# First loads in smaller pieces, and the first convolution ahead of a weight split, in a four-network transformer kernel

## Chip, cores and metric

The kernel runs on one core of one Trainium2 chip. The metric is device time in microseconds (us); three runs gave 1028.97, 1029.12 and 1029.18, median 1029.12. Engines are called by the profile's names: PE is TensorE, DVE is VectorE, ACT is ScalarE, POOL is GpSimd, SP is the engine that issues most transfers.

## What is computed

Two transformer stages over 256 tokens of 1024 features, in float32. The first stage is a short-convolution mixer, a SwiGLU network, sliding-window attention and a second SwiGLU network; the second stage is a SwiGLU network, a mixture of latent attention and retention, and a last SwiGLU network. Each branch sits between RMS norms and is added to the residual. The change lies in the mixer, at the very start:

```python
# h: (256, 1024); w_in: (1024, 3 * 1024); conv_w: 3 taps for each feature
n = h * rsqrt(mean(h * h) + 1e-6) * pre_norm
b, c, u = split(n @ w_in, 3)          # gate, carrier, value
y = b * causal_conv(c * u, conv_w)    # three taps along the tokens
h = h + rmsnorm(y @ w_out, post_norm)
```

(The names b, c, u are this sketch's own.)

## The kernel before

**Tiling.** The 256 tokens are two row tiles of 128 (t = 0 and 1). Weights come from memory as a stream of chunks, each 128 x 1024 floats (512 KB). To keep float32 accuracy at a faster matmul rate, each chunk is split in two: ACT copies it, rounded, to `w_high` (`split_high`, L1370) and DVE subtracts, giving `w_low` (`split_low`, L1693). The activations are split the same way (`xTh`, `xTl`). A product then takes three passes, high x high, high x low and low x high (L2097, L2098, L2101 for the mixer's inputs; L2108, L2112, L2116 elsewhere). The split chunks go round a ring of 12 slots.

**The mixer** has 8 blocks of 128 features (384 weight columns each, three chunks), and for each row tile and block: G, the input product; a gate copied by ACT (L1484) and multiplied by DVE (L1849, `act`); T, two transposes on PE (L2125) followed by the convolution, ACT's copy `cv` (L1495), ACT's first tap `yT` (L1500), DVE's other taps (L1873) and its product with the gate (L1875); Y, the split of the result into `aTh` (ACT, L1517) and `aTl` (DVE, L1884); D, the output product.

**The start.** Block 0's input product (`first`, L2142) does not use the split: it multiplies the unsplit turned x (`hg`, after the norm's gain, L1716) with unsplit weights `first_w` in plain float32, 8 k tiles of 384 columns for each row tile, while the first chunks are loaded and split. SP issues the loads in this order: left half of x of tile 0 (256 KB), chunks 0 and 1 of `first_w`, right half of x of tile 0, chunk 2 of `first_w`, x of tile 1, then `raw` chunk 0, h of tile 0 (needed for the norm's root), `raw` chunks 1 to 3, four `early` chunks, h of tile 1. ACT issues one load, `consts` (the identity for the transposes and the gains and taps together, 109.5 KB). Before the data is there PE runs 11 matmuls on a zeroed tile (`WARM_UPS`, L2131). DVE waits for `consts` and then for each half of x; `first` waits for a half of `hg` and for each chunk of `first_w`.

**The order of the work** is written by hand: one function calls the same steps for all engines and each engine takes its own part. Chunks are numbered from 0 after those of `first_w`; chunks 0 to 2 are block 1's input weights, 3 is block 0's output weights, 4 to 6 are block 2's input. The transposes of block 0 are not a step of their own on PE but stand inside block 1's input product, ahead of the k tile that `TURN_IN_PRODUCT` names for the row tile:

```python
if ph.mixer and b == 1 and kt == TURN_IN_PRODUCT[t]:
    turn_gated(t, 0, ph)
```

SP reloads a `raw` buffer once the chunk in it is split (L1116).

Of the kernel before, what the change touches and what calls it, by code (L numbers as in the profile page):

```python
# [35 lines left out]
P = 128  # L36
D = 1024
# [83 lines left out]
TURN_IN_PRODUCT = (2, 2)  # L121
FIRST_TURN = 4
TABLES_AFTER = 24
WARM_UPS = 11
# [99 lines left out]
def walk_first_block(step):  # L224

    step("turn", 0, 0)
    step("first", 0)
    step("parts", 0, 0)
    step("turn", 1, 0)
    step("first", 1)  # L230
    split(step, 0)
    step("norm", 0)
    split(step, 1)
    step("G", 0, 0, 0)
    split(step, 2)
    step("high", 3)
    step("T", 0, 0, 0)
    step("low", 3)
    step("high", 4)
    step("Y", 0, 0, 0)  # L240
    step("low", 4)
    step("high", 5)


def walk_second_block(step):

    step("G", 0, 1, 0)
    step("low", 5)
# [517 lines left out]
def build(nc, x_in, x_turned, stream, consts_in, table_in, pos_in, posts_in, out):  # L766
    with ExitStack() as ctx:
# [144 lines left out]
        first_loaded = [sem(f"first_loaded{i}") for i in range(FIRST)]  # L912
        first_done1, warm_ready = sem("first_done1"), sem("warm_ready")
        h_loaded = rows2("h_loaded")
        xt_left, xt_right, xt1_loaded = sem("xt_left"), sem("xt_right"), sem("xt1_loaded")
# [4 lines left out]
        d_quarter, end_m, end_r, end_w = sem("d_quarter"), sem("end_m"), sem("end_r"), sem("end_w")  # L920
# [9 lines left out]
        halo_zero = sem("halo_zero")  # L930
# [3 lines left out]
        q_done0 = sem("q_done0")  # L934
# [7 lines left out]
        x_done0, u_done0 = sem("x_done0"), sem("u_done0")  # L942
# [19 lines left out]
        e_ready, lg_ready = sem("e_ready"), sem("lg_ready")  # L962
# [73 lines left out]

        def branch_done(eng, t, k, half):
# [23 lines left out]
        def proj_done(eng, j, t):  # L1061
            if t == 0:
                eng.wait_ge(q_done0, j + 1)
# [3 lines left out]
        def x_product(eng, i, t):  # L1067
            if t == 0:
                eng.wait_ge(x_done0, i + 1)
# [11 lines left out]
        def _(sp):  # L1081
            def start(ph):
                def first_weights(i):
                    sp.dma_start(first_w[:, i * CHUNK:(i + 1) * CHUNK], stream[i]).then_inc(first_loaded[i], 16)
# [68 lines left out]
        def _(pool):  # L1153
# [8 lines left out]
            def start(ph):  # L1162
                link(pool.memset(half_neg, -0.5))
                link(pool.memset(one_neg, -1.0))
                for i in range(3):
                    pool.memset(cv[i][:, 0:2], 0.0).then_inc(halo_zero, 1)
# [33 lines left out]
            def log_decays():  # L1200
# [13 lines left out]
                pool.tensor_scalar(lg, lg_p, -1.0, None, ALU.mult).then_inc(lg_ready, 1)  # L1214
# [116 lines left out]
            def finish(ph):  # L1331
# [4 lines left out]
                for half in range(2):  # L1336
                    pool.wait_ge(h_ready[0], 2 * FFN4.index + half + 1)
                    weighted(0, slice(512 * half, 512 * half + 512)).then_inc(end_w, 1)
                pool.wait_ge(end_m, 1)
                pool.tensor_tensor(rr[0], ms[0], half_neg[:, 0:1], ALU.pow).then_inc(end_r, 1)  # L1340
                pool.wait_ge(end_w, 1)
# [1308 lines left out]
```

## Time and profile before

| | |
|---|---|
| median of three runs | 1029.12 us |
| the profiled execution, its own time | 1029.98 us |
| its span in the profile | 1028.2 us |
| PE busy | 1020.1 us, 99% of the span |
| DVE busy | 684.2 us, 67% |
| ACT busy | 567.0 us, 55% |
| PE's share of the chain that ended last | 96% |
| DMA, mean over the span | 198 GB/s |

The span is what the profile shows between the first and the last instruction; 1.8 us of the profiled execution's time lie outside it. Matmuls are pipelined and their ends are modelled, so PE's busy time hides short pauses; the starts of successive matmuls show them better. An answer for a stretch gives each engine's busy time in it, the granted clock of PE and the share and rate of the transfers.

### The profile page before, as it was taken

Reading aid. Unit: us, or ns where it says so; the run is one execution under the profiler, and the core shown is the slowest. Engines: PE = TensorE matmul, PEld = TensorE weight load, DVE = VectorE, ACT = ScalarE, POOL = GpSimd, SP = SyncE. Lnnn points to the kernel's source line nnn. Section 1 sums busy time; section 2 is a strip of 40 time slices with the busy share of each in tenths; the row PEclk is TensorE's granted clock in tenths of the full one; section 3 lists DMA queues with packets and bytes.
Section 4 is the critical chain, followed back from the end, with each engine's and each line's share of the span. In section 5 each row is a group of like instructions: output and inputs, shape, how many; then the busy total and the mean of one; then the engine's idle time right before and its main releaser. Section 6 shows DMA issues by size and latency. Waiting matters only on the chain.

```text
span 1028.2 us, 14332 instructions
## 1 busy us (share of the span) xinstructions
PE 1020.1 (99%) x4783; PEld 839.0 (82%) x4783; DVE 684.2 (67%) x1034; ACT 567.0 (55%) x925; POOL 137.1 (13%) x219
## 2 busy tenths in 40 slices
PE   9999999999999999999999999999999999999997
PEld 6999888888877778888888888888887688888886
DVE  5777856656788985656668565656787685655643
ACT  5665654545567864444556454454676854454542
POOL 1100450000143152000014000000400220000002
PEclk9999999999999999999999999999999999999999
DMA  9575577566643467667576775757643355757551
GB/s 364 174 238 187 184 226 242 179 226 200 211 145 126 146 225 249 217 196 243 178 235 210 233 222 188 245 176 243 207 168 122 98 171 176 239 184 238 187 175 46
DMA packets 104174, 203.56 MB, mean 198 GB/s; under 512 B 52976, under 2 KB 57472, under 8 KB 104128
## 3 DMA queue, kind: packets, MB, share of 16 engines
q1 hardware_dynamic: 101952, 197.44, 59.0%
q0 software_dynamic: 1888, 5.17, 1.8%
q8 instruction: 25, 0.41, 0.2%
q10 hardware_dynamic: 288, 0.37, 0.1%
q14 instruction: 21, 0.17, 0.1%
HBM read 187.20 MB, written 1.05 MB: 183 GB/s over the span
## 4 chain that ended last, share of the span: by engine, by line
PE 96%; DVE 1%; ACT 1%; DMA 0%; POOL 0%; issue 0%; POOLq 0%; DVEq 0%; SPq 0%; ACTq 0%
PE pG L2108 16%; PE pG L2116 16%; PE pG L2112 16%; PE pD L2108 11%; PE pD L2112 11%; PE pD L2116 11%; PE pG L2097 2%; PE pG L2101 2%; PE pG L2098 2%; PE pT L2125 1%; PE pD L2142 1%; PE pD L2101 1%; PE pD L2097 1%; PE pD L2098 1%; PE pG L2422 1%; PE pG L2125 1%
## 5 line engine op out<-in xcount | busy, mean ns | idle before, releaser
L1693 DVE TENSOR_TENSOR w_low<-raw,w_high 128x1024 fp32r<-128x1024 f32 x340 | 410.3, 1225 | 195.8 <-ACT w_high L1370 185.7
L1370 ACT ACTIVATE w_high<-raw 128x1024 fp32r<-128x1024 f32 x340 | 354.7, 1056 | 207.0 <-PE pG L2116 135.9
L2108 PE MATMUL pG<-w_high,xTh 128*128 128x512 f32 x712 | 220.0, 390 | 0.0
L2112 PE MATMUL pG<-w_high,xTl 128*128 128x512 f32 x712 | 219.6, 389 | 0.0
L2116 PE MATMUL pG<-w_low,xTh 128*128 128x512 f32 x712 | 219.4, 390 | 0.2 <-DVE w_low L1693 0.2
L2116 PEld LDWEIGHTS pG<-w_low,xTh 128*128 128x128 f32 x712 | 133.6, 188 | 28.2 <-DVE w_low L1693 0.6
L2112 PEld LDWEIGHTS pG<-w_high,xTl 128*128 128x128 f32 x712 | 133.6, 188 | 28.1 <-DVE xTl L1739 0.2
L2108 PEld LDWEIGHTS pG<-w_high,xTh 128*128 128x128 f32 x712 | 133.3, 188 | 27.3
L1484 ACT ACTIVATE gate<-pG,stat 128x256 f32<-128x256 f32 x102 | 48.4, 474 | 140.1 <-PE pG L2116 124.0
L2108 PE MATMUL pD<-w_high,aTh 128*128 128x512 f32 x348 | 107.8, 391 | 0.0
L2116 PE MATMUL pD<-w_low,aTh 128*128 128x512 f32 x348 | 107.5, 390 | 0.0
L2112 PE MATMUL pD<-w_high,aTl 128*128 128x512 f32 x348 | 107.4, 390 | 0.0
L1856 DVE SCALAR_TENSOR_TENSOR act<-pG,stat,gate 128x256 f32<-128x256 f32 x88 | 43.9, 499 | 70.7 <-ACT gate L1484 70.4
L2116 PEld LDWEIGHTS pD<-w_low,aTh 128*128 128x128 f32 x348 | 65.2, 188 | 14.2 <-DVE w_low L1693 0.7
L2112 PEld LDWEIGHTS pD<-w_high,aTl 128*128 128x128 f32 x348 | 65.3, 188 | 13.8
L2108 PEld LDWEIGHTS pD<-w_high,aTh 128*128 128x128 f32 x348 | 64.8, 188 | 12.1
L2108 PE MATMUL pD<-w_high,xTh 128*128 128x512 f32 (+1 forms) x144 | 47.1, 408 | 0.0
L2112 PE MATMUL pD<-w_high,xTl 128*128 128x512 f32 (+1 forms) x144 | 44.3, 389 | 0.0
L1259 POOL TENSOR_SCALAR stat<-stat 128x1 f32<-128x1 f32 x8 | 2.8, 356 | 308.9 <-ACT junk L1466 308.7
L2116 PE MATMUL pD<-w_low,xTh 128*128 128x512 f32 (+1 forms) x144 | 44.0, 387 | 0.0
L1266 POOL DMA_DIRECT2D xF<-hg x32 | 18.0, 568 | 174.1 <-DVE hg L1768 173.9
L1509 ACT ACTIVATE aTh<-aF 128x256 fp32r<-128x256 f32 x80 | 32.9, 411 | 11.3 <-DMA aF<-aB 10.3
(312 smaller groups left out, 1112.9 us busy)
## 6 DMA issues: line engine op xcount, KB each, us to landing
raw<-in_stream SPq DMA_DIRECT2D x340, 512.0 KB, 4.6
aF<-aB SPq DMA_DIRECT2D x320, 32.0 KB, 2.6
post<-in_posts POOLq DMA_DIRECT2D x5, 512.0 KB, 4.7
early<-in_stream SPq DMA_DIRECT2D x4, 512.0 KB, 13.1
xF<-hg SPq DMA_DIRECT2D x32, 64.0 KB, 2.5
xF<-hg POOLq DMA_DIRECT2D x32, 64.0 KB, 2.3
first_w<-in_stream SPq DMA_DIRECT2D x3, 512.0 KB, 5.8
h<-in_x SPq DMA_DIRECT2D x2, 512.0 KB, 11.9
```

The lines of the kernel that those rows point to most:

```text
L1370: sc.activation(w_high[:, slot(static):slot(static) + CHUNK], raw_of(static), ACT.Copy).then_inc(w_high_done, 1)
L1484: sc.activation(gate[t][:], gate_bank(ph, t, b)[:, 0:256], ACT.Copy if ph.mixer else ACT.Silu, scale=rr[t]).then_inc(gate_ready[t], 1)
L1509: sc.activation(act_parts(ph, t, b)[0][:].rearrange("p k (a r) -> p k a r", a=4), turned_act(ph, t, b), ACT.Copy).then_inc(ah_ready[t], 1)
L1693: ve.tensor_tensor(w_low[:, slot(static):slot(static) + CHUNK], raw_of(static), w_high[:, slot(static):slot(static) + CHUNK].bitcast(F32), ...
L1856: ve.scalar_tensor_tensor(dst, up, rr[t], by, ALU.mult, ALU.mult).then_inc(act_ready[t], 1)
L2097: pe.matmul(dst, ah, hi, start=start, stop=False)
L2098: pe.matmul(dst, ah, lo, start=False, stop=False)
L2101: return pe.matmul(dst, al, hi, start=False, stop=stop)
L2108: pe.matmul(dst, ah, w_high[:, where:where + n], start=start, stop=False)
L2112: pe.matmul(dst, al, w_high[:, where:where + n], start=False, stop=False)
L2116: mm = pe.matmul(dst, ah, w_low[:, where:where + n], start=False, stop=stop)
L2125: return pe.transpose(dst, src, ident)
```

## The change

- SP's first loads become smaller: x of tile 0 as two quarters (128 KB each) and its right half; `first_w` as six pieces of 512 columns (256 KB) in place of three chunks; x of tile 1 as two halves. The identity (64 KB) is loaded by SP between the halves of x of tile 1, and ACT's own load is the gains and taps alone (45.5 KB).
- DVE makes the left half of `hg` in two quarters. PE starts `first` with the first quarter and the first piece. DVE makes `hg` of tile 1 ahead of `xTl` of tile 0. The first block still takes tile 0 whole and then tile 1.
- 9 zero matmuls in place of 11.
- The transposes of block 0, tile 0, stand ahead of k tile 3 instead of k tile 2.
- On ACT the high part of chunk 3 comes behind the convolution's `cv` and `yT`, and that of chunk 4 behind `aTh`; chunk 5 follows the gate.
- Some semaphores are merged into one with counts (`proj_done0`, `end_weights`, `halo_and_logs`), which frees the numbers for the new pieces; the order of what is waited for stays.

```diff
-TURN_IN_PRODUCT = (2, 2)
+TURN_IN_PRODUCT = (3, 2)
-WARM_UPS = 11
+WARM_UPS = 9
+PIECE = 512
...
 def walk_first_block(step):
 
-    step("turn", 0, 0)
+    step("opening", 0)
     step("first", 0)
+    step("opening", 1)
+    step("first", 1)
     step("parts", 0, 0)
-    step("turn", 1, 0)
-    step("first", 1)
     split(step, 0)
     step("norm", 0)
     split(step, 1)
     step("G", 0, 0, 0)
     split(step, 2)
-    step("high", 3)
     step("T", 0, 0, 0)
-    step("low", 3)
-    step("high", 4)
+    split(step, 3)
     step("Y", 0, 0, 0)
-    step("low", 4)
-    step("high", 5)
+    split(step, 4)
...
     step("G", 0, 1, 0)
-    step("low", 5)
+    split(step, 5)
     split(step, 6)
...
-                sp.dma_start(xt[0][:, 0:512], x_turned[0, :, 0:512]).then_inc(xt_left, 16)
+                left_quarter, second_quarter, right_half = slice(0, 256), slice(256, 512), slice(512, D)
+                load_x(0, left_quarter, xt_first)
                 first_weights(0)
                 first_weights(1)
-                sp.dma_start(xt[0][:, 512:D], x_turned[0, :, 512:D]).then_inc(xt_right, 16)
+                load_x(0, second_quarter, xt_second)
                 first_weights(2)
-                sp.dma_start(xt[1][:], x_turned[1]).then_inc(xt1_loaded, 16)
+                load_x(0, right_half, xt_right)
+                for i in (3, 4, 5):
+                    first_weights(i)
+                load_x(1, slice(0, 512), xt1_loaded)
+                sp.dma_start(consts[:, C_ID:C_FEATS], consts_in[:, C_ID:C_FEATS]).then_inc(ident_loaded, 16)
+                load_x(1, right_half, ident_loaded)
...
-                sc.dma_start(consts[:, 0:C_ROPE], consts_in[:, 0:C_ROPE]).then_inc(ident_loaded, 16)
+                sc.dma_start(consts[:, C_FEATS:C_ROPE], consts_in[:, C_FEATS:C_ROPE]).then_inc(xt_first, 16)
...
-                ve.wait_ge(ident_loaded, 16)
...
+            def opening(t, ph):
+                if t == 0:
+                    ve.wait_ge(xt_first, 32)
+                    gained_quarter(0, 0).then_inc(warm_ready, 1)
+                    ve.wait_ge(xt_second, 16)
+                    gained_quarter(0, 1).then_inc(hg_ready[0], 1)
+                    ve.wait_ge(xt_right, 16)
+                else:
+                    ve.wait_ge(xt1_loaded, 16)
+                    gained_quarter(1, 0).then_inc(warm_ready, 1)
+                    gained_quarter(1, 1).then_inc(hg_ready[1], 1)
+                    ve.wait_ge(ident_loaded, 32)
+                gained(t, GAIN[0], 1, xt[t][:, 512:D])
...
-                pe.wait_ge(ident_loaded, 16)
 
             def first(t, ph):
 
+                pe.wait_ge(warm_ready, t + 2)
                 for kt in range(KT):
-                    if kt % 4 == 0:
-                        pe.wait_ge(hg_ready[t], kt // 4 + 1)
+                    if kt in (2, 4):
+                        pe.wait_ge(hg_ready[t], kt // 2)
                     if t == 0:
-                        for i in range((kt * MIX.cols + CHUNK - 1) // CHUNK, ((kt + 1) * MIX.cols - 1) // CHUNK + 1):
+                        for i in range((kt * MIX.cols + PIECE - 1) // PIECE, ((kt + 1) * MIX.cols - 1) // PIECE + 1):
                             pe.wait_ge(first_loaded[i], 16)
...
+                if t:
+                    pe.wait_ge(ident_loaded, 32)
```

How the instructions stand on an engine before and in the changed kernel, at three places. SP's queue at the start, before (`xt_56` is x of tile 0, `xt_57` of tile 1, `h_58` the residual of tile 0):

```order
L1092 DMA xt_56<-in_x_turned 128x512
L1084 DMA first_w<-in_stream 128x1024 x2
L1095 DMA xt_56<-in_x_turned 128x512
L1084 DMA first_w<-in_stream 128x1024
L1097 DMA xt_57<-in_x_turned 128x1024
L1087 DMA raw<-in_stream 128x1024
L1090 DMA h_58<-in_x 128x1024
```

and now:

```order
L1089 DMA xt_56<-in_x_turned 128x256
L1086 DMA first_w<-in_stream 128x512 x2
L1089 DMA xt_56<-in_x_turned 128x256
L1086 DMA first_w<-in_stream 128x512
L1089 DMA xt_56<-in_x_turned 128x512
L1086 DMA first_w<-in_stream 128x512 x3
L1089 DMA xt_57<-in_x_turned 128x512
L1107 DMA consts<-in_consts 128x128
L1089 DMA xt_57<-in_x_turned 128x512
L1092 DMA raw<-in_stream 128x1024
```

Six loads stood ahead of the first `raw` chunk; now twelve do, with 64 KB more (the identity, which ACT's load gave up).

ACT from the high part of chunk 1 to the gate of block 1, before:

```order
L1370 ACTIVATE w_high<-raw 128x1024
L1484 ACTIVATE gate_88<-pD,stat 128x256
L1370 ACTIVATE w_high<-raw 128x1024 x2
L1495 ACTIVATE cv_96<-pT 128x128
L1500 ACTIVATE yT_99<-cv_96,consts 128x128
L1370 ACTIVATE w_high<-early 128x1024
L1517 ACTIVATE aTh_80<-yT_99 128x128
L1370 ACTIVATE w_high<-early 128x1024
L1484 ACTIVATE gate_88<-pG,stat 128x256
```

and now:

```order
L1380 ACTIVATE w_high<-raw 128x1024
L1493 ACTIVATE gate_88<-pD,stat 128x256
L1380 ACTIVATE w_high<-raw 128x1024
L1504 ACTIVATE cv_96<-pT 128x128
L1509 ACTIVATE yT_99<-cv_96,consts 128x128
L1380 ACTIVATE w_high<-raw 128x1024
L1526 ACTIVATE aTh_80<-yT_99 128x128
L1380 ACTIVATE w_high<-early 128x1024
L1493 ACTIVATE gate_88<-pG,stat 128x256
```

Each of the splits of chunks 3, 4 and 5 stands one place later against the convolution and the gate; DVE's order in this stretch is the same in both.

PE in block 1's input product of tile 0 (three rows are one k tile), now:

```order
L2122 MATMUL pG0<-w_high_50,xTh0_52 128x384
L2123 MATMUL pG0<-w_low_51,xTh0_52 128x384
L2126 MATMUL pG0<-w_high_50,xTl0_54 128x384
L2150 MATMUL pT0<-consts_63,gate0_88 128x128
L2150 MATMUL pT0<-consts_63,act0_90 128x128
```

Three k tiles stand ahead of the two transposes, where two did; five follow instead of six.

## Rows read from the trace of the kernel before

**Rows 1.** The page: busy time, and the chain that ended last, by engine.

```profile
PE 1020.1 (99%) x4783; PEld 839.0 (82%) x4783; DVE 684.2 (67%) x1034; ACT 567.0 (55%) x925; POOL 137.1 (13%) x219
...
PE 96%; DVE 1%; ACT 1%; DMA 0%; POOL 0%; issue 0%; POOLq 0%; DVEq 0%; SPq 0%; ACTq 0%
```

**Rows 2.** The chain of waits up to 24 us: start us, us, what.

```profile
1.20 4.99 DMA first_w<-in_stream
6.18 0.14 issue
6.32 10.93 PE pD L2142 x32
...
22.84 0.27 DVE act L1849
23.16 0.44 PE pT L2125 x2
```

**Rows 3.** Stretches: engines busy us (count), PEclk, DMA share, GB/s.

```profile
2.00:2.50 0.50, 0.50 (x3) 0.21 (x2) 0.00 (x0) 0.47 (x1) 0.00 (x0) 1.00 0.59 87
10.00:15.00 5.00, 5.00 (x17) 3.02 (x16) 2.52 (x3) 2.78 (x6) 1.15 (x2) 1.00 1.03 410
...
23.15:29.00 5.85, 5.84 (x32) 5.54 (x33) 5.42 (x9) 4.76 (x12) 2.11 (x3) 1.00 0.77 305
29.00:40.00 11.00, 11.00 (x64) 10.57 (x63) 8.54 (x17) 7.22 (x15) 1.18 (x1) 1.00 0.37 121
```

**Rows 4.** Transfers issued in the first 12 us: KB each, median us to landing.

```profile
first_w<-in_stream SPq DMA_DIRECT2D x3, 512.0 KB, 5.8
...
xt<-in_x_turned SPq DMA_DIRECT2D x2, 256.0 KB, 5.1
xt<-in_x_turned SPq DMA_DIRECT2D x1, 512.0 KB, 7.3
consts<-in_consts ACTq DMA_DIRECT2D x1, 109.5 KB, 4.3
```

**Rows 5.** Timeline, start: start us, us, engine, line, count, [idle before <-releaser].

```profile
0.74 0.40 SPq L1092 DMA_DIRECT2D xt<-in_x_turned  x1
1.19 4.87 PE L2131 MATMUL pD<-warm 128*128 128x512 bf16 x11 [1.19 <-DVE warm L1702]
5.10 0.69 DVE L1716 TENSOR_TENSOR hg<-xt,consts 128x512 f32<-128x512 f32 x1 [3.97 <-DMA consts<-in_consts]
...
12.01 1.06 ACT L1370 ACTIVATE w_high<-raw 128x1024 fp32r<-128x1024 f32 x1 [2.48 <-DMA raw<-in_stream]
```

**Rows 6.** Timeline of PE alone, 6.2 to 9 and 9 to 12 us.

```profile
6.32 2.86 PE L2142 MATMUL pD<-first_w,hg 128*128 128x384 f32 x7 [0.26 <-DMA first_w<-in_stream]
...
8.69 3.71 PE L2142 MATMUL pD<-first_w,hg 128*128 128x384 f32 x11
```

**Rows 7.** Timeline, PE, 17 to 24 us.

```profile
18.14 0.27 PE L2125 MATMUL pT<-consts,gate 128*128 128x128 f32 x1
...
21.51 0.62 PE L2108 MATMUL pD<-w_high,aTh 128*128 128x512 f32 x2
```

**Rows 8.** Timeline, ACT, 14 to 24 us.

```profile
16.14 2.05 ACT L1370 ACTIVATE w_high<-raw 128x1024 fp32r<-128x1024 f32 x2
18.56 0.28 ACT L1495 ACTIVATE cv<-pT 128x128 f32<-128x128 f32 x1 [0.37 <-PE pT L2125]
...
20.62 1.05 ACT L1370 ACTIVATE w_high<-early 128x1024 fp32r<-128x1024 f32 x1
```

**Rows 9.** Timeline, DVE, 14 to 24 us.

```profile
16.80 0.34 DVE L1849 SCALAR_TENSOR_TENSOR act<-pD,stat,gate 128x128 f32<-128x128 f32 x1
...
20.29 1.22 DVE L1693 TENSOR_TENSOR w_low<-raw,w_high 128x1024 fp32r<-128x1024 f32 x1
21.63 1.22 DVE L1693 TENSOR_TENSOR w_low<-early,w_high 128x1024 fp32r<-128x1024 f32 x1
22.76 0.34 DVE L1849 SCALAR_TENSOR_TENSOR act<-pG,stat,gate 128x128 f32<-128x128 f32 x1
```

More of the change, by code:

```diff
@@ L911, in build @@
         w_freed = sem("w_freed")
-        first_loaded = [sem(f"first_loaded{i}") for i in range(FIRST)]
+        first_loaded = [sem(f"first_loaded{i}") for i in range(FIRST * CHUNK // PIECE)]
         first_done1, warm_ready = sem("first_done1"), sem("warm_ready")
         h_loaded = rows2("h_loaded")
-        xt_left, xt_right, xt1_loaded = sem("xt_left"), sem("xt_right"), sem("xt1_loaded")
+        xt_first, xt_second, xt_right, xt1_loaded = sem("xt_first"), sem("xt_second"), sem("xt_right"), sem("xt1_loaded")
         ident_loaded, tables_loaded = sem("ident_loaded"), sem("tables_loaded")
@@ L1035, in moved_block, with x_count @@
             return network(ph) * (ph.nb - 1) + b + t + shift * (RING // (ph.cg + ph.kd))
+        def x_count(i):
+            return 3 + i + (1 if i < 3 else 2)
         def branch_done(eng, t, k, half):
@@ L1711, in low, with gained_quarter @@
                 split_low(c, c)
+            def gained_quarter(t, quarter):
+                cols = slice(256 * quarter, 256 * quarter + 256)
+                g = feats[:, 2 * quarter:2 * quarter + 2].unsqueeze(2).broadcast_to([P, 2, P])
+                return ve.tensor_tensor(hg[t][:, cols].rearrange("p (k r) -> p k r", k=2), xt[t][:, cols].rearrange("p (k r) -> p k r", k=2),
+                                        g, ALU.mult)
             def gained(t, col, half, src):
@@ L1745, in turn @@
                     sinks()
-                if p == 0:
-                    for half in range(2):
-                        ve.wait_ge(xt1_loaded if t else (xt_left, xt_right)[half], 16)
-                        gained(t, GAIN[p], half, xt[t][:, 512 * half:512 * half + 512])
-                elif (t, p) not in RIGHT_ONLY:
+                if (t, p) not in RIGHT_ONLY:
                     for half in range(2):
                         gained_half(t, p, GAIN[p], half)
+            def opening(t, ph):
[11 more added lines that the diff above has]
+                gained(t, GAIN[0], 1, xt[t][:, 512:D])
             def left(t, ph):
@@ L2084, in RL @@
                                  xTh[t][:, 4:8, :].rearrange("p k r -> p (k r)").bitcast(F32), ALU.subtract).then_inc(catT_ready[t], 1)
-            steps = dict(start=start, low=low, R=refill, left=left, turn=turn, parts=parts, second=second, second_low=second_low, spread=spread, gain=gain, rest=rest, finish=finish, tail=tail, join=join, G=G, V=V, T=T, Y=Y,
+            steps = dict(start=start, low=low, R=refill, opening=opening, left=left, turn=turn, parts=parts, second=second, second_low=second_low, spread=spread, gain=gain, rest=rest, finish=finish, tail=tail, join=join, G=G, V=V, T=T, Y=Y,
                          rope=rope, QKT=QKT, S=S, N=N, AT=AT, LAT=LAT, KPE=KPE, U=U, RROPE=RROPE, RSUM=RSUM, MT=MT, MS=MS, MN=MN, VC=VC, RT=RT, RM=RM, GNvar=GNvar, GNout=GNout,
```

52 lines of the change are left out of this document (26 added, 26 removed).

## The prediction

> **What bounds the kernel now.** I read the page first: PE is busy 99% of the span and is 96% of the chain that ended last [rows 1]. The change touches only the first 30 us, so next the chain of waits there [rows 2]. It begins with a transfer: the first chunk of `first_w`, issued at 1.20 us, lands at 6.19. At 6.32 PE starts the first product, and then works nearly without a pause, but for one place: the chain leaves PE after the transposes of block 0, goes through the convolution and the splits on DVE, and comes back at 23.16, when `act` of block 1 is ready. How long PE stood there: between the transposes at 18.14 and the output product at 21.51 [rows 7] lie the two transposes (0.11 each by their starts) and six k tiles of three matmuls, so a k tile takes (21.51 - 18.36) / 6 = 0.52, a matmul of 384 columns 0.175 and one of 512 columns 0.233. The output product has six of the latter, so PE was free at 22.91 and waited 0.25. Behind it the stretches show PE busy 5.84 of 5.85 us and 11.00 of 11.00 [rows 3]. So whatever the change does to the moment when PE takes up the transposes of block 1 (23.16) goes through to the end of the kernel, us for us, and nothing else in it does.
>
> **The measure.** A measurement of this kernel can tell about 0.2% from no change, that is 2.06 us. The first product cannot begin before the zero matmuls are done, at 5.0 (below). The whole prize is thus 1.3 us plus the 0.25 us wait.
>
> **Part 1: when the first product starts.** The transfers move 410 GB/s once they run (10 to 15 us [rows 3]), 0.41 MB a us; at 2 to 2.5 us it is 87 GB/s [rows 3]. The start waits for three things.
> (a) The zero matmuls: 11 starting at 1.19 take 4.87 us with the last one's modelled end [rows 5], 0.43 each, so two fewer end 0.85 us earlier, 5.85 - 0.85 = 5.00.
> (b) The first quarter of `hg`. DVE started at 5.10, when `consts` had landed (4.3 us after an issue at 0.74, the moment of SP's first) [rows 4, 5]. In front of it there are now 128 KB less of x and 64 KB less of `consts`: 0.19 MB, 0.47 us at 410 GB/s, so 4.6. A quarter takes half of 0.69 [rows 5]: 4.97.
> (c) The first piece. Ahead of 6.19 lay 0.90 MB (half of x, `consts`, one chunk); now 0.44 MB (a quarter, 45.5 KB, one piece). 0.46 MB less are 1.1 us: 5.1. With the 0.13 us from landing to start that PE needed before, the first product starts at about 5.2.
> The bounds: 5.0, the zero matmuls' end, and 6.3, if landing goes by a fixed latency and not by bytes. I take 5.2, since the steady part of the landings goes by bytes.
>
> **Part 2: how much earlier it ends.** The granted clock column says 1.00 from 2 us on [rows 3], but the spacing says otherwise: 512 columns every 0.43 us is the 1.2 GHz level. Each k tile of the first product is recorded as two matmuls. From 8.69 us 11 of them take 3.71, the last one's modelled 0.49 within: (3.71 - 0.49) / 10 = 0.322 each. The first seven: the last starts at 6.32 + 2.86 - 0.49 = 8.69, five steps of 0.322 back is 7.08, so the first one took 0.76 [rows 6]. PE thus went from the lower to the upper level (2.4 GHz) at about 7.0 us, having worked on the zero matmuls since 1.19. If that moment stays, the product's first us run at half rate: started at 5.2, its first record takes 0.76, the second 0.644 (to 6.60), three are done at 7.16. Before, one was done at 7.08. The gain is 2 x 0.322 - 0.08 = **0.56 us**. Had PE the upper level from the start, it would be the whole 1.1 us.
> The rest of the pieces must keep ahead. At 0.64 us for 256 KB they land at 5.75 (piece 1), 6.05 (second quarter), 6.7, 7.35 (right half), 8.0, 8.6, 9.25, then x of tile 1 at 9.9 and 10.7. PE wants piece 1 at 6.6, piece 2 at 7.5, piece 3 and the right half of `hg` (7.35 + 0.69) at 8.8, the last pieces at 9.4 and 10.1, tile 1 from 11.3 on. At least 0.65 us is in hand everywhere, so nothing waits. `raw` chunk 0 lands, by bytes, at 11.96 as before (ACT took it at 12.01 [rows 5]); behind it nothing changes.
> A rule of the Trainium skill speaks against the pieces. The page "DMA: Bandwidth & Descriptors", section "Rules for kernel authors", wants 1 MiB or more in one transfer for the full rate and calls transfers under 64 KB mostly overhead; the features' 45.5 KB are such a one, and by this page's 2 us of fixed cost for a transfer, were it not overlapped, SP's six further ones would cost 12 us (an estimate). The trace agrees only in part, since 512 KB transfers already run at 410 GB/s here.
>
> **Part 3: from there to 23.16.** The transposes of block 0 stood behind two k tiles and started at 18.14 [rows 7]; now a third stands ahead, 0.52 us. New start: 18.14 - 0.56 + 0.52 = **18.10**, 0.04 earlier. The gain of part 2 is spent on the later place. `act` of block 0 was ready at 16.80 + 0.34 = 17.14 [rows 9], so it binds neither place.
> Behind it the chain is the same on DVE: taps, `low` of chunk 3 at 20.29, `low` of chunk 4 at 21.63, `act` at 22.76 [rows 9]. ACT did the high parts of chunks 2 and 3 back to back from 16.14 to 18.19 and then stood until `cv` at 18.56 [rows 8]. The high part of chunk 3 is moved out of this free stretch, behind `yT`: 19.2 to 20.2, just ahead of DVE's 20.29. That of chunk 4 moves behind `aTh`: it takes the place of the one that started at 20.62 and took 1.05, ends at 21.67, and DVE's split of it can begin at 21.70 instead of 21.63. That is **+0.07 us**. The convolution itself does not come sooner for being put first, since ACT was waiting for PE and not PE for ACT [rows 8].
> Sum at 23.16: -0.04 + 0.07 = **+0.03 us**. PE reaches the place 0.56 us earlier and waits there 0.25 + 0.56 + 0.03 = 0.84 us. Behind it ACT has the high part of chunk 5 one place later than before, with some 0.2 us in hand on DVE and PE; it costs nothing while that cover lasts, and up to 0.2 us if not.
>
> **Part 4: the rest.** The merged semaphores count the same events in the same order; nothing new is waited for: 0. DVE's `xTl` of tile 0 comes behind the two halves of x of tile 1, at about 12.1 instead of 8.8, and is wanted by PE at 16.5: 0. PE's wait for the identity stands at 16.5, with the landing at about 10: 0. SP has six issues more ahead of the `raw` chunks, 0.46 us each (from 0.74 to 1.20 [rows 2, 5]), 2.8 us in all, hidden by the backlog of transfers (the third rival).
>
> The profiled execution had 1029.98 us and a span of 1028.2; the sum gives 1030.0 for it. The median of the runs lies 0.86 below the profiled one; +0.03 on 1029.12 is below a tenth of what can be told, and I forecast **1029.1 us**, chance 0.50.
>
> **Rivals.**
> 1. The gain passes. If the product starts at 5.2 or sooner and PE has the upper level by then, its end is 1.1 us earlier instead of 0.56; 0.59 of it (0.52 for the later transposes, 0.07 for ACT) is spent and 0.5 is left: **1028.6**; with a start at 5.0 and ACT's 0.07 not binding, 1.3 - 0.5 = 0.8, 1028.3. For it: the moment of the rise is a single one in a single execution. Against: rows 6 show it after 6.3. The Trainium skill, "TensorE: Matmul & The Clock Gate", section "Part 1: The HAM clock gate", has this moment shift by half a us from run to run, which speaks for it; no run here shows the shift. Chance 0.24.
> 2. The landing does not come sooner, so the change does not do what it says. At 2 to 2.5 us the transfers are 0.59 busy and move 87 GB/s [rows 3]: the first packets wait on latency. If the first piece lands at 6.2 as before, the gain is 0 and the later place and ACT's order remain: +0.59, **1029.7**. Chance 0.17.
> 3. The number of transfers binds. If `raw` chunks land by their issue, the six issues make each 2.8 us late. DVE's `low` of chunk 1, done just ahead of 16.80 [rows 9], comes at 19.6; PE wants it at 17.6 for its third k tile and has the transposes at 20.1, 2.0 us late. Half of that may be made up behind: +1.0 to +2.0, **1030.6**. Against: a landing 7.3 us after the issue [rows 4] is queueing, not issue. Chance 0.05.
> 4. Slower: the clock. Between the zero matmuls' end and the first product PE may stand longer than the 0.3 us of before, and the lower level may last on. Decides: whether the level rises near 7 us. From the first zero matmul to the rise it took 5.8 us; if the count starts anew with the product at 5.2, the rise is at 11.0, nine records pass at 0.644 and 23 at 0.322, and the product ends at 18.5 against 17.06 (31 steps of 0.322 behind 7.08). With the later transposes and ACT's order that is +2.0: **1031.1**, and over 0.2% with any further wait. Chance 0.04.
>
> **How the numbers follow.** The forecast's case spans 1028.8 to 1029.5. The range takes in rivals 1 and 2 with their bounds (5.0 and 6.3 for the start, 0.2 for ACT's later place) and leaves out rivals 3 and 4: 1028.3 to 1030.0. Faster by over 2.06 us needs more than the prize holds: 0.01. Slower by so much is half of rival 4 and what I have not seen: 0.03. The rest, 0.96, is no change that can be told.
>
> **What would show it.** The first `first` matmul at 5.0 to 5.4; the step from 0.644 to 0.322 us near 7 us; the last of them at about 16.2 instead of 16.76; transposes of block 0 at 18.1, those of block 1 at 23.2 with PE standing 0.8 us ahead of them; ACT's high part of chunk 4 ending at 21.7 and DVE beginning its low part right behind it. The forecast is wrong if the transposes of block 1 start before 22.9 or after 23.5, or if PE pauses anywhere in the first product.

## The result, and the profile after

The changed kernel takes **1030.45 us** (median of 20 runs, 1030.13 to 1031.32), the kernel before 1029.12 beside it (20 runs, 1028.73 to 1029.46): +1.33 us, a ratio of 1.0014 with a 95% interval of 1.0008 to 1.002. That is slower by less than the 2.06 us that were called distinguishable, but it lies outside the range of the prediction, which had 1029.1 (1028.3 to 1030.0). The profiled execution took 1031.06 us with a span of 1029.2.

The page of the changed kernel (its busy lines and the chain by engine) looks like [rows 1]; transfers have gone from 0% of the chain to 1%.

```profile
PE 1019.5 (99%) x4781; PEld 838.6 (81%) x4781; DVE 684.1 (66%) x1036; ACT 565.8 (55%) x925; POOL 138.6 (13%) x219
...
PE 96%; DVE 1%; ACT 1%; DMA 1%; POOL 0%; issue 0%; SPq 0%; POOLq 0%; DVEq 0%; ACTq 0%
```

The chain of waits of the changed kernel up to 25 us (start us, us, what) names the piece: it no longer begins with the first weights but with the third piece, issued at 2.60.

```profile
2.60 5.80 DMA first_w<-in_stream
8.40 0.14 issue
8.54 9.27 PE pD L2167 x28
...
21.70 1.13 DVE w_low L1702
22.83 0.20 DVE aTl L1909
23.03 1.23 DVE w_low L1702
24.26 0.27 DVE act L1874
24.53 0.04 issue
24.57 0.44 PE pT L2150 x2
```

PE's timeline in the changed kernel shows what lies before and behind (start us, us, engine, line, operation, count, and in brackets the idle time ahead).

```profile
3.72 1.49 PE L2156 MATMUL pD<-warm 128*128 128x512 bf16 x3
5.00 1.82 PE L2167 MATMUL pD<-first_w,hg 128*128 128x384 f32 x4
8.54 4.76 PE L2167 MATMUL pD<-first_w,hg 128*128 128x384 f32 x14 [1.73 <-DMA first_w<-in_stream]
...
18.84 0.44 PE L2122 MATMUL pG<-w_high,xTh 128*128 128x384 f32 x1
...
19.47 0.27 PE L2150 MATMUL pT<-consts,gate 128*128 128x128 f32 x1
...
24.57 0.33 PE L2150 MATMUL pT<-consts,gate 128*128 128x128 f32 x1 [0.29 <-DVE act L1874]
```

The product starts at 5.00 instead of 6.32, does two k tiles (four records), and then stands 1.73 us for weight piece 2. The transposes of block 0 are at 19.47 (18.14 in [rows 7]), those of block 1 at 24.57 (23.16 in [rows 2]): +1.41. On ACT the high part of `raw` chunk 0 starts at 13.91 instead of 12.01 [rows 5], 1.90 late:

```profile
13.91 1.06 ACT L1380 ACTIVATE w_high<-raw 128x1024 fp32r<-128x1024 f32 x1 [3.50 <-DMA raw<-in_stream]
...
20.51 1.05 ACT L1380 ACTIVATE w_high<-raw 128x1024 fp32r<-128x1024 f32 x1
21.73 0.31 ACT L1526 ACTIVATE aTh<-yT 128x128 fp32r<-128x128 f32 x1 [0.18 <-DVE yT L1900]
21.95 1.05 ACT L1380 ACTIVATE w_high<-early 128x1024 fp32r<-128x1024 f32 x1
```

Both come from one cause, which the stretches show (columns as in rows 3; the DMA share and GB/s are the last two). The changed kernel:

```profile
2.00:3.00 1.00, 1.00 (x4) 0.44 (x3) 0.00 (x0) 0.47 (x1) 0.00 (x0) 1.00 0.86 253
3.00:4.00 1.00, 1.00 (x4) 0.32 (x3) 0.40 (x1) 0.00 (x0) 0.00 (x0) 1.00 1.04 345
4.00:5.00 1.00, 1.00 (x4) 0.49 (x2) 0.02 (x1) 0.00 (x0) 0.00 (x0) 1.00 0.74 170
5.00:6.00 1.00, 1.00 (x3) 0.57 (x2) 0.00 (x0) 0.00 (x0) 0.00 (x0) 1.00 0.95 284
6.00:8.00 2.00, 0.81 (x3) 0.19 (x1) 0.43 (x1) 0.63 (x1) 0.00 (x0) 1.00 0.95 302
8.00:10.00 2.00, 1.46 (x5) 0.88 (x6) 0.69 (x1) 0.23 (x1) 0.00 (x0) 1.00 0.94 325
10.00:12.00 2.00, 2.00 (x8) 1.08 (x7) 0.23 (x1) 0.40 (x1) 1.26 (x1) 1.00 1.08 419
```

The kernel before, the same stretches up to 10 us:

```profile
2.00:3.00 1.00, 1.00 (x4) 0.44 (x3) 0.00 (x0) 0.47 (x1) 0.00 (x0) 1.00 0.59 108
3.00:4.00 1.00, 1.00 (x4) 0.32 (x3) 0.00 (x0) 0.00 (x0) 0.00 (x0) 1.00 0.87 300
4.00:5.00 1.00, 1.00 (x4) 0.30 (x3) 0.00 (x0) 0.00 (x0) 0.00 (x0) 1.00 1.05 412
5.00:6.00 1.00, 1.00 (x3) 0.15 (x1) 0.69 (x1) 0.18 (x1) 0.00 (x0) 1.00 1.03 408
6.00:8.00 2.00, 1.74 (x5) 1.07 (x5) 0.00 (x0) 0.45 (x1) 0.00 (x0) 1.00 1.04 419
8.00:10.00 2.00, 2.00 (x8) 1.16 (x7) 1.29 (x2) 0.63 (x1) 0.40 (x1) 1.00 1.02 416
```

From 2 to 4 us the changed kernel moves 190 KB more than the kernel before. From 4 to 10 us it moves 782 KB less. Over 2 to 10 us that is 2,306 KB instead of 2,898, and the missing 592 KB are 1.4 us at 410 GB/s. The rest of the 1.9 is unevenness. Each of these transfers is spread over the 16 DMA engines and has landed when the last of the 16 parts has. The parts of `raw` chunk 0 land at 12.76 on average instead of 11.39 (+1.37), the last of them at 13.88 instead of 11.98. The lag stays: the last part comes 0.93 us behind the 14th at this chunk and 0.95 behind it at 25 us, where the two lay 0.2 apart before.

Part of the lost bytes is idle engines (share 0.74 at 4 to 5 us), the larger part is packets that take longer. Packets of 2 KB took 84 ns in the kernel before and 102 on average in the changed one from 6 to 8 us, by single ones of up to 1,048 ns.

### The profile page after: what moved, and what is told of

Its sections match the earlier page's. It is cut to its first block, busy times and chain, and to the rows that moved or that the text cites. A ratio compares the mean times of both kernels' runs of the same rounds, so it can differ in the third digit from the quotient of the medians.

```text
span 1029.2 us, 14335 instructions
## 1 busy us (share of the span) xinstructions
PE 1019.5 (99%) x4781; PEld 838.6 (81%) x4781; DVE 684.1 (66%) x1036; ACT 565.8 (55%) x925; POOL 138.6 (13%) x219
## 4 chain that ended last, share of the span: by engine, by line
PE 96%; DVE 1%; ACT 1%; DMA 1%; POOL 0%; issue 0%; SPq 0%; POOLq 0%; DVEq 0%; ACTq 0%
PE pG L2141 16%; PE pG L2133 16%; PE pG L2137 16%; PE pD L2133 11%; PE pD L2137 11%; PE pD L2141 11%; PE pG L2122 2%; PE pG L2126 2%; PE pG L2123 2%; PE pT L2150 1%; PE pD L2167 1%; PE pD L2126 1%; PE pD L2123 1%; PE pD L2122 1%; PE pG L2449 1%; PE pG L2150 1%
```

## The experiments

All against the kernel before on the same chip. The interval of each ratio is about 0.0009 wide to either side, 0.9 us, so a difference of a few tenths between two kernels rests on the traces, not on their times. And a trace is one execution. The changed kernel, the loads alone (2) and the kernel with only the transposes put back (2) have the very same loads, and `raw` chunk 0 lands at 13.88, 13.24 and 13.83 in their traces. In two traces of the kernel before and that of the order alone (1), again with the same loads, it lands at 11.98, 11.69 and 11.67. A landing that differs by 0.6 us among the cut loads, or by 0.3 among the old ones, shows nothing by itself.

**1. The order of work without the loads.** The kernel before with the later transposes and ACT's new order:

```
-TURN_IN_PRODUCT = (2, 2)
+TURN_IN_PRODUCT = (3, 2)
...
-    step("high", 3)
     step("T", 0, 0, 0)
-    step("low", 3)
-    step("high", 4)
+    split(step, 3)
     step("Y", 0, 0, 0)
-    step("low", 4)
-    step("high", 5)
+    split(step, 4)
...
-    step("low", 5)
+    split(step, 5)
```

> The kernel before with nothing changed but the place of block 0's transposes (behind three k tiles instead of two) and ACT's order of the splits of chunks 3 to 5. If the order costs what the prediction's part 3 says (0.52 us for the place, 0.07 for ACT), block 1's transposes come at 23.75 instead of 23.16 and the time is 1029.7. If the whole loss of the change is a matter of the loads, it is 1029.1.

1029.95 us (1029.66 to 1030.94) beside 1029.35: **+0.60**, ratio 1.0006 (0.9997 to 1.0015). Its trace is best read against a second profile of the kernel before (experiment 7), whose product starts at the same moment. PE, the second profile of the kernel before:

```profile
6.02 5.18 PE L2142 MATMUL pD<-first_w,hg 128*128 128x384 f32 x14
...
17.89 0.27 PE L2125 MATMUL pT<-consts,gate 128*128 128x128 f32 x1
...
22.91 0.33 PE L2125 MATMUL pT<-consts,gate 128*128 128x128 f32 x1
```

PE, the order alone:

```profile
6.00 5.17 PE L2139 MATMUL pD<-first_w,hg 128*128 128x384 f32 x14
...
18.39 0.27 PE L2122 MATMUL pT<-consts,gate 128*128 128x128 f32 x1
...
23.50 0.33 PE L2122 MATMUL pT<-consts,gate 128*128 128x128 f32 x1 [0.30 <-DVE act L1846]
```

The transposes of block 0 are 0.50 later and those of block 1 0.59. The prediction had 0.52 for the place and 0.07 for ACT's order. This half was right by the traces; by time alone +0.60 can't be told from nothing.

**2. The loads without the order of work.** The changed kernel with both of the above put back:

> The changed kernel with the old place of the transposes and ACT's old order: the loads, the quarters of hg and the 9 zero matmuls alone. Loads theory (raw chunk 0 lands near 13.9 us instead of 12.0, everything behind it late): DVE's act of block 0 stays at 18.7, the transposes come right behind it at 19.05 instead of 19.47, and the time is 0.4 to 0.5 below the changed kernel's, 1029.9 to 1030.0. If the order had been the loss, it would be near 1028.6.

1030.54 us (1030.05 to 1031.23): **+1.19**, ratio 1.0012 (1.0003 to 1.0021). `raw` chunk 0 lands at 13.24 (11.98 before), and PE stands twice in its first product, 0.42 and 0.64 us. So the loads alone lose nearly what the changed kernel loses (by 1.19 against 1.33), clear of no change; their gain at the start is gone. The two halves together (0.60 + 1.19) are more than the changed kernel's 1.33. In the loads alone the way from the transposes of block 0 to those of block 1 takes 5.46 us, in the changed kernel 5.11: when `raw` chunk 3 is late, the old order on ACT holds the convolution behind it. To see that by itself, the changed kernel with only the transposes put back:

```
-TURN_IN_PRODUCT = (3, 2)
+TURN_IN_PRODUCT = (2, 2)
```

> The changed kernel with the transposes of block 0 back at the place of before (2, 2), its loads and its ACT order (convolution ahead of the split) kept. If the order on ACT helps once raw chunk 3 is late (its T of block 0 to T of block 1 took 5.11 us in the changed kernel, 5.46 with the old order), the time is 0.9 us over before, 0.3 under the kernel with the new loads alone. If the two orders are worth the same, it stands at the new loads alone, 1.2 over before; if the later transposes are no part of the loss, at the changed kernel's 1.3.

1030.24 us beside 1029.3, ratio 1.0007 (0.9998 to 1.0016). (One of its 12 runs took 2676.77 us, a disturbance that no other run showed; without it the median is 1030.17, +0.87.) Transposes at 19.05 and 24.20, 5.16 apart. The sign is as the first theory has it: convolution first is worth about 0.3 us behind late loads (5.46 - 5.16, and 1.19 - 0.87), but by time alone it can't be told from nothing.

**3. Which of the cuts costs?** The loads alone, with the weights again in three whole chunks (`PIECE = 1024`), x still in quarters:

> As loads_alone, but first_w comes in three whole chunks with 4 KB rows again; x of tile 0 stays in quarters (nine transfers ahead of raw chunk 0 instead of twelve; six before). Row theory (2 KB rows out of 4 KB rows of the stream move at 0.3 MB/us with single packets far over the usual 84 ns): the stall is gone, raw chunk 0 lands at 12.1 to 12.5, the first product starts at 5.0 to 5.6 and does not pause, time 1028.6 to 1029.0. Count theory (the number of transfers and SP's issues delay the rest): half of the delay stays, raw chunk 0 near 13, time near 1029.6.

1029.98 us beside 1029.35: +0.63, ratio 1.0006 (0.9997 to 1.0015); `raw` chunk 0 at 13.06, PE stood 1.26 us for the second chunk. That is what the theory of the count has, and not that of the rows. And the reverse, six pieces, but x of tile 0 in halves:

> As loads_alone (six pieces of weights, old order), but the left half of x of tile 0 comes in one transfer with 2 KB rows, so no transfer has 1 KB rows. whole_chunks showed that the quarters of x by themselves cost about 0.6 us (raw chunk 0 at 13.1). If the two parts add up, this one has raw chunk 0 at about 12.8 and 1029.9; if any small rows do it and the pieces are the larger part, 13.2 to 13.5 and 1030.2; if the quarters alone do it, 12.0 and 1029.2.

1030.70 us beside 1029.28: +1.42, ratio 1.0014 (1.0005 to 1.0023); chunk 0 at 13.63. With neither cut (three chunks, halves of tile 0; x of tile 1 in halves with the identity between them, the features alone on ACT's queue and nine zero matmuls kept):

> As whole_chunks, but x of tile 0 in halves as in the kernel before: neither quarters nor pieces. What is left of the change's loads: x of tile 1 in halves with the identity between them, the features alone on ACT's queue, 9 zero matmuls, hg of tile 1 ahead of xTl of tile 0. If small rows are the loss: raw chunk 0 at 12.0, first product at 5.4 to 5.7 for want of 64 KB of identity ahead of it, time 1028.9 to 1029.3 (before: 1029.35 on this chip). If the number of transfers is (eight ahead of raw chunk 0, six before), 12.5 and 1029.6.

1029.47 us beside 1029.28: +0.19, ratio 1.0003 (0.9994 to 1.0012); chunk 0 at 12.31. Against this last kernel the quarters alone cost 0.44 us more and the pieces alone 1.23. They do not add up: with the pieces in, the quarters bring nothing more (1.19 with them, 1.42 without). Of these four kernels only the two with the pieces stand clear of no change by their times; the pieces are the larger part.

**4. Is it the place of the pieces in memory?** A piece is 2 KB out of each row of 4 KB, a quarter of x 1 KB out of 4. The loads alone with the pieces each together in memory, and the kernel of whole chunks with the quarters so:

```
-sp.dma_start(first_w[:, cols], stream[i * PIECE // CHUNK][:, i * PIECE % CHUNK:i * PIECE % CHUNK + PIECE])
+sp.dma_start(first_w[:, cols], first_in[i])
...
```

> As loads_alone, but the six pieces of weights lie each together in memory (256 KB without a gap) instead of as halves of 4 KB rows; sizes, rows of 2 KB in SBUF, order and number are the same. If the gaps in memory make the packets slow, raw chunk 0 comes at 12.9 to 13.2 instead of 13.9 and 13.2, packets back at 84 ns, and the time falls by 0.5 or more. If the size of a row does it, nothing changes: 1030.4 to 1030.6.

> As whole_chunks, but the two quarters of x of tile 0 lie each together in memory (128 KB without a gap) instead of as quarters of 4 KB rows. If the gaps make them slow, raw chunk 0 comes at 12.2 instead of 13.1 and the time is 1029.2 or less. If it is the 1 KB rows, or the number of transfers, it stays at 1029.8 to 1030.0.

1030.27 us (+0.99, 1.0 to 1.0018) and 1030.23 us (+0.95, 0.9999 to 1.0017), beside 1029.28; chunk 0 at 13.00 and 12.65. With the gaps it was +1.19 and +0.63. The landing of 13.00 lies where the theory of the gaps had it (12.9 to 13.2), but it is not apart from the 13.24 to 13.88 of the same loads with gaps by more than these differ among themselves, and the time did not fall by the 0.5 us that was named. So the gaps are not the main cause; a few tenths can't be excluded.

A third way to ask, six weight transfers of 64 partitions with whole rows of 4 KB:

```
-    cols = slice(i * PIECE, (i + 1) * PIECE)
+    cols, rows = slice(i // 2 * CHUNK, (i // 2 + 1) * CHUNK), slice(64 * (i % 2), 64 * (i % 2) + 64)
...
```

> As loads_alone, but the six weight transfers are 64 partitions each with whole 4 KB rows, two for a chunk: the same number of transfers, issues and bytes as the changed kernel, rows twice as long. Row theory: raw chunk 0 at 12.1 to 12.6 and 1028.7 to 1029.1, like whole_chunks. Count theory: raw chunk 0 near 13.9 and 1029.9 to 1030.0, like loads_alone.

1033.91 us beside 1029.35 (5 runs, 1032.29 to 1035.54): +4.56, ratio 1.0045 (1.0031 to 1.0059). It answers nothing on the question, since with these transfers in the queue all packets were slow: from 4 to 12 us those of 4 KB took 256 to 313 ns on average instead of 159, and those of 2 KB, which belong to x with its 128 partitions, 140 instead of 84. The engines were full (share 1.03):

```profile
8.00:10.00 2.00, 1.14 (x2) 0.00 (x0) 0.69 (x1) 0.22 (x1) 0.00 (x0) 1.00 1.03 213
```

**5. The number of transfers or the size of rows?** The kernel before with six tiny transfers between its first six, nothing cut:

```
 sp.dma_start(xt[0][:, 0:512], x_turned[0, :, 0:512]).then_inc(xt_left, 16)
+sp.dma_start(tiny[0:16, 0:64], consts_in[0:16, 0:64]).then_inc(xt1_loaded, 16)
 first_weights(0)
+sp.dma_start(tiny[0:16, 64:128], consts_in[0:16, 0:64]).then_inc(xt1_loaded, 16)
...
```

> The kernel before with six tiny transfers (16 rows of 256 bytes, 4 KB each) put between its six opening loads on SP's queue; no large transfer is cut. Theory of the count (each further transfer ahead of the raw chunks costs them about 0.25 us): raw chunk 0 lands about 1.5 us later, at 13.2 to 13.6 instead of 11.98, and the kernel takes 0.8 to 1.4 us more. Theory of the short rows: the loads keep their rates (about 410 GB/s from 5 to 10 us), raw chunk 0 lands by 12.3, and the time stands within 0.3 us of before.

1030.1 us beside 1029.3: **+0.80**, ratio 1.0008 (1.0 to 1.0017). Six transfers of 4 KB each, and against 410 GB/s the stretches from 4 to 8 us lose 140, 60 and 158 KB (over 2 to 4 us it moved 200 KB more than the kernel before, so that by 10 us it is 0.2 MB behind, about 0.5 us):

```profile
4.00:5.00 1.00, 1.00 (x3) 0.30 (x2) 0.69 (x1) 0.28 (x1) 0.00 (x0) 1.00 0.84 270
5.00:6.00 1.00, 1.00 (x3) 0.15 (x1) 0.00 (x0) 0.35 (x1) 0.00 (x0) 1.00 0.87 350
6.00:8.00 2.00, 1.13 (x5) 0.68 (x4) 0.00 (x0) 0.00 (x0) 0.00 (x0) 1.00 1.03 331
```

The product starts at 6.93, for want of chunk 0 of `first_w`: 15 of the 16 engines had delivered their part of chunk 0 by 5.10, the last one at 6.80. The changed kernel has the same picture at its piece 2 (15 parts by 6.91, the last at 8.40). `raw` chunk 0 lands at 12.60. The time was as the count has it, the landing was 0.6 sooner than it had it. The other half, three weight transfers of twice the rows:

```
-sp.dma_start(first_w[:, i * CHUNK:(i + 1) * CHUNK], stream[i])
+sp.dma_start(first_w[:, i * CHUNK:(i + 1) * CHUNK].rearrange("p (c n) -> p c n", c=2),
+             first_in[i].rearrange("c p n -> p c n"))
...
```

> The kernel before with its three weight transfers still three, but each of 256 rows of 2 KB (out of two areas in memory) in place of 128 rows of 4 KB; x and the queue as before. Theory of the short rows: a packet of 2 KB does not fill an engine as one of 4 KB does, 4 to 10 us move about 300 GB/s, raw chunk 0 lands at about 13, and the kernel takes 0.6 us more or over. Theory of the count: six transfers as before, raw chunk 0 at 12.0 to 12.3, the time within 0.2 us of before.

1029.64 us: +0.34, ratio 1.0003 (0.9994 to 1.0012); chunk 0 at 12.26, 322 and 342 GB/s at 5 to 6 and 6 to 8 us. The landing is the count's, the time lies between the two theories and can't be told from nothing. The number of transfers counts, with an interval whose lower end is no change; that the rows count too is not shown. That 0.80 + 0.34 = 1.14 is about the 1.19 of the loads alone may be chance, with intervals of 0.9 us.

**6. Does a transfer cost the engines, or does SP hand over too little ahead?** The same six tiny transfers, but among the `raw` chunks:

> The kernel before with the six tiny transfers (4 KB each) between and behind the raw chunks, not between the first six loads. Theory of too short a lead: at that time 3 MB and more are queued, so they cost nothing beyond their bytes; raw chunk 0 at 12.0, the time within 0.2 us of before (they cost 0.8 us among the first loads). Theory that each transfer costs the engines 0.13 us or so wherever it stands: the chunks behind come later by 0.1 to 0.7 us, and the kernel takes 0.3 to 0.8 us more.

1029.43 us beside 1029.23: +0.20, ratio 1.0002 (0.9993 to 1.0011); chunk 0 at 11.70 and `raw` chunks 1 to 3 at 14.33, 15.66 and 17.01, 0.08 to 0.20 later than in the second profile of the kernel before, at 400 GB/s and more. So a tiny transfer costs the engines some 0.05 us there at most, against about 0.13 among the first loads. Then the loads alone with pieces 1, 3 and 5 handed over by ACT:

```
 sc.dma_start(consts[:, C_FEATS:C_ROPE], consts_in[:, C_FEATS:C_ROPE]).then_inc(xt_first, 16)
+for i in (1, 3, 5):
+    cols = slice(i * PIECE, (i + 1) * PIECE)
+    sc.dma_start(first_w[:, cols], stream[i * PIECE // CHUNK][:, i * PIECE % CHUNK:i * PIECE % CHUNK + PIECE]).then_inc(first_loaded[i], 16)
...
```

> The new loads with the old order of work (the kernel 1.19 us over before), with weight pieces 1, 3 and 5 handed over by ACT behind the features, and the rest by SP as before: the same transfers, rows and bytes. Theory that SP hands over too little ahead (one transfer each 0.47 us, while what is queued is short): with two issuers the engines are full from 3 us on, raw chunk 0 lands at 12.2 to 12.6 instead of 13.24, PE's stall before its third k tile is under 0.5 us, and the kernel takes 0.5 to 1.2 us less than with the new loads alone, so 0.0 to 0.7 over before, perhaps less than before. Theory that each short row or each transfer costs the engines: raw chunk 0 stays at 13.0 to 13.5 and the time at 1.0 to 1.3 over before.

1031.02 us beside 1029.23 (1030.65 to 1032.63): **+1.79**, ratio 1.0021 (1.0012 to 1.003). All six weight pieces were issued by 3.6 us, and yet the engines were idle and slow in the same stretches:

```profile
4.00:5.00 1.00, 1.00 (x3) 0.15 (x1) 0.23 (x1) 0.00 (x0) 0.00 (x0) 1.00 0.72 236
5.00:6.00 1.00, 1.00 (x3) 0.61 (x3) 0.00 (x0) 0.00 (x0) 0.00 (x0) 1.00 0.89 224
```

`raw` chunk 0 landed at 13.18, as in the loads alone, though it was issued at 5.88 instead of 7.02, and PE stood 1.56 us before its third k tile. My theory that SP's 0.47 us per issue leaves the engines without work is refuted; the time is above the other theory's range too (+1.0 to +1.3). The changed kernel's own trace says the same: by 4.0 us 1.6 MB were issued and 0.6 MB moved, and yet the next stretch moves 170 GB/s with a share of 0.74. The Trainium skill, "Perfetto Trace Analysis", section "DMA Optimizations", holds out that spreading transfers over the issuing engines may help where the generation of descriptors is the bottleneck; by this run the spreading did not help: it measured 0.6 us more than the loads alone, less than the two intervals can tell apart.

**7. The clock, and the kernel before once more.** The kernel of experiment 3 with neither cut had its profile with TensorE at the lower level (1.2 GHz) for long. PE's timeline there:

```profile
5.85 5.51 PE L2166 MATMUL pD<-first_w,hg 128*128 128x384 f32 x9 [0.64 <-DMA first_w<-in_stream]
```

The same for the kernel with the features first, further below, whose first product has the same instructions:

```profile
4.29 0.81 PE L2131 MATMUL pD<-warm 128*128 128x512 bf16 x3
5.55 5.78 PE L2141 MATMUL pD<-first_w,hg 128*128 128x384 f32 x16 [0.45 <-DMA first_w<-in_stream]
```

In the first one the starts of the nine records lie (5.51 - 0.49) / 8 = 0.63 us apart, the 1.2 GHz level; in the second those of the 16 lie 0.35 apart with two short pauses within, the 2.4 GHz level. There the last three zero matmuls are already at 0.21 instead of 0.43, so the step came at about 4.0 us. In the kernel with neither cut it came at about 10.6, and that execution took 1031.88. With 11 zero matmuls instead of nine:

> The kernel with whole chunks and halves of x, features alone and identity late (0.19 us over before, its profile with TensorE at the lower level until about 10.5 us), with 11 zero matmuls again instead of 9. If the two matmuls hold the clock's rise: it rises by 7.1 us in the profile, no run lies over 1030.2, the median is 1029.2 to 1029.5. If they have nothing to do with it: single runs 1 to 2.5 us over the median come here too, or came there by chance and neither kernel has them in every second set.

1029.27 us beside 1029.23 (1028.96 to 1030.37): +0.04, ratio 1.0001 (0.9992 to 1.001), and the upper level from the first record, at 5.68. The widest run is 1.1 over the median, where the kernel with nine had 2.4; it lies above the 1030.2 that was named. Runs further over their median than 1.1 stand only in kernels with nine zero matmuls: two of the kernel with neither cut, three of the two issuers (1.4 to 1.6), one of the 64 partitions (1.6) and one of six pieces with halves of x (1.2), beside the disturbance of experiment 2. The other profile with a late step, between 8.3 and 10.2 us, is that of the 64 partitions, nine zero matmuls too. In both PE stood (0.6 and 1.0 us) between the last zero matmul and the product with the lower level still on. With eleven, experiment 5's tiny transfers made PE stand 0.87 us, and its product had the upper level at once. That fits the two zero matmuls as what keeps the step from coming late, but the eight other profiles with nine have it between 4.2 and 7.0, and a rare event could have missed a set of 11 runs; it stays likely, not shown. The kernel before with only its constants split (features alone, identity behind x of tile 1):

> The kernel before with only the change's split of the constants: the features alone (8 KB or so) on ACT's queue, the identity from SP behind x of tile 1; the weights and x are loaded as before, in whole chunks and halves. Seven transfers ahead of the raw chunks. The first product starts when its zero matmuls are through and x's first half and chunk 0 are there, about 5.9 to 6.3. Either theory: raw chunk 0 within 0.3 us of before, and the time from 0.3 us less to 0.2 us more than before.

1029.45 us beside 1029.3: +0.15, ratio 1.0002 (0.9993 to 1.001), although its profile has the product at 5.55 and the transposes of block 1 at 22.59. That is the execution whose step came at 4.0, and at 1029.27 it is 0.18 under its median: a lucky one. (The features are 45.5 KB, not the 8 that this expectation gives.) Last, the kernel before unchanged:

> The kernel before, unchanged, for a second profile. If the first profiled execution (0.86 us over the median) had its excess in the opening, the block transposes stand 0.4 to 0.9 us earlier here (first one at 17.3 to 17.8 instead of 18.14) where this execution lies near the median. If the opening is the same in each execution, they stand at 18.0 to 18.3 whatever the time.

1029.2 us; its profiled execution took 1029.63, 0.43 over the median where the first one was 0.86 over. Product at 6.02 instead of 6.32, transposes of block 1 at 22.91 instead of 23.16. So 0.25 of the 0.35 between the two lies in the opening, and the first profile, on which the prediction rests, was of an unlucky execution. The transposes of block 0 stand at 17.89, between the two ranges that were named: the opening differs, but by less than the whole excess.

## Why the prediction was wrong

Against the second profile of the kernel before the account of the changed kernel closes. The last record of the first product starts at 17.33 instead of 16.52: +0.80. The transposes of block 0: +1.57, of which 0.52 is their later place, 0.15 PE's wait at the third k tile, whose `low` (chunk 1) ended at 18.77 for a matmul at 18.84, and 0.11 the slower first matmul behind this wait (0.28 to the next one instead of 0.17). The transposes of block 1: +1.66. Some 0.2 of it is made up between 237 and 336 us, so the prediction's "us for us" is not quite kept (the same comparison at transposes near 351 and 552 us gives +1.48 and +1.46), and the spans differ by 1.4, the medians by 1.33.

- **Part 1, the start**: right in kind. The zero matmuls set it, as its bound (a) said: 5.00 instead of 5.2. The first quarter of `hg` began at 3.60, a whole us sooner than the 4.6 worked out, since the quarter and the features landed 2.5 and 2.8 us after their issue; the first piece landed at 4.09 for the 5.1 worked out.
- **Part 2, the clock**: the step came at 5.7 us, not at 7.0, so the premise of rival 1 nearly held: only the first of the 32 records ran at the lower level (0.64 us). It brought nothing, because PE had run out of weights. The moment itself is luck: over the profiles here it lies between 4.0 and 10.6.
- **Part 2, "at least 0.65 us is in hand everywhere, so nothing waits", is the step that failed**, and with it "`raw` chunk 0 lands, by bytes, at 11.96 as before". It spread the pieces at 0.64 us for 256 KB, the 410 GB/s of transfers of 512 KB at 10 to 15 us. Piece 1 and the second quarter kept to it (5.54 and 6.21, worked out 5.75 and 6.05). Piece 2 landed at 8.40 instead of 6.7, and all that follows is late by the same 1.7 to 1.9: 9.70 for 8.0, 10.37 for 8.6, 11.05 for 9.25, 13.88 for 11.96. The sum had to use another rate, 170 to 325 GB/s from 4 to 10 us, and a term for the slowest engine, 0.5 us. In its place the prediction had -0.56 us for the loads; measured alone they cost 1.19.
- **The rule weighed there** was dismissed on the row of 512 KB transfers, which said nothing of smaller ones. The Trainium skill's rule in "DMA: Bandwidth & Descriptors", section "Rules for kernel authors", pointed to the right side. The fixed cost of 2 us for a transfer, which that page fits in "Anatomy of one DMA — SWDGE (gpsimd) path" to transfers issued from GpSimd, would have given 12. The runs, with transfers issued from SP, show about 0.13 each for the tiny ones (0.80 by six).
- **Part 3**: right, and measured by itself. +0.59 predicted for place and order, +0.59 in the trace and +0.60 in time (experiment 1), the latter within an interval of 0.9 that makes the agreement to 0.01 luck. In the changed kernel 5.11 us lie between the two transposes, 0.09 more than before, for 0.07.
- **Part 4**: "hidden by the backlog" failed by its result. The six issues more did cost, by the landings. Rival 3 named that consequence, `raw` chunks late and +1.0 to +2.0, and had 0.05; its price came true, its mechanism (landing by SP's issue) did not, since with two issuers they were as late. Rival 2's +0.59 is what the order alone gives, but its condition did not hold: the first piece landed at 4.09, not at 6.2.
- **Rival 4** is no fancy: experiment 7 has an execution in which the lower level lasted to 10.6 us, where the rival had 11.0, at 2.4 us over its median. It wasn't what the changed kernel did.

What is shown is that the loads do it (experiment 2), by landing later (the traces). What stays open is why the short transfers run slowly in the first 8 to 10 us and no longer from 10 us on, where the packets of 2 KB in the changed kernel are back at 84 ns. It goes with the number of transfers there (5, and 3 in kind); that the shortness of rows adds to it is not shown. It is not mainly their place in memory (4), not SP's rate of issue (6), and not a price of each transfer wherever it stands (6). A single engine that lags makes 0.5 of the 1.9 us. Such lags are not the cut transfers' alone: in the kernel with neither cut one packet of 4 KB took 1,649 ns. Which resource holds that engine, no run told.

No version beat the kernel before: the best, with the loads whole and 11 zero matmuls, measured 1029.27 to its 1029.23.

## What to carry to other kernels

Before cutting the first loads so that work can start sooner, take the price of a transfer from transfers of that size at that time of the program, not from the steady rate; here the cuts cost 1.2 us at the end, for a start that came 1.0 to 1.3 us sooner. Look for the consumer that needs the last byte of the queue: a cut gains at the head once, and delays everything behind. And separate an edit's halves on the chip early: the part worked out from rows of the same instructions was right within what the traces can tell, the part extrapolated from another size was off by 1.9.

## What the runs showed of the hardware

- With weight transfers of 64 partitions and rows of 4 KB in the queue the engines moved 213 to 256 GB/s from 4 to 12 us, busy all the while; with 128 partitions they moved 410. Packets of the other transfers between them were slowed too.
- A DMA engine that falls behind stays behind: in the changed kernel the part that came last at `raw` chunk 0 still comes 0.95 us behind the 14th at 25 us, and each transfer lands with it.
- TensorE's step to the upper level came at about 4.0, at 5.7, at 6.9 to 7.1 and at about 10.6 us in profiles whose zero matmuls all began at 1.19, while the granted clock column read 1.00 in each; only the spacing of the matmuls shows it. The Trainium skill, "TensorE: Matmul & The Clock Gate", section "Part 1: The HAM clock gate", lets this moment shift by half a us; the runs here show over 6.
- The opening of the same kernel differs between two executions by 0.3 us at the first product, which goes through to the end. A prediction of tenths of a us needs more than one profile.
